# Two mixture-of-experts stages written out, with ring slots in turn, whole weight tiles, combination products moved earlier and GpSimd's share of the work moved to other engines

## The chip, the cores and the metric

One core of one Trainium2 chip runs the whole program. The metric is the device time of one execution in microseconds (us). The kernel before took 2744.36 us, the median of 3 runs (2743.35 to 2745.78).

## The reference, cut to what matters

A six-layer network on 256 tokens of width 1024, all in float32. The first two layers (a convolution mixer, then a differential attention beside a Hyena mixer) each end in an expert-choice feed-forward, the second four in a dense one. The change touches the two expert stages alone:

```python
def expert_choice_ffn(h, w_router, w_gate, w_up, w_down):
    aff = jax.nn.softmax((h @ w_router).astype(jnp.float32), axis=-1)
    g, idx = lax.top_k(jnp.swapaxes(aff, 1, 2), cap)          # cap = 32 tokens for each of 16 experts
    xe = jax.vmap(lambda hb, ib: hb[ib])(h, idx)
    a = jnp.einsum('becd,edf->becf', xe, w_gate)
    up = jnp.einsum('becd,edf->becf', xe, w_up)
    y = jnp.einsum('becf,efd->becd', jax.nn.silu(a) * up, w_down) * g[..., None].astype(h.dtype)
    return jax.vmap(lambda ib, yb: jnp.zeros((n, d), h.dtype).at[ib.reshape(-1)].add(yb.reshape(-1, d)))(idx, y)
```

In layer 0 it runs over two token sets (the sequence and its context, `ns = 2`) with the same weights, in layer 1 over one (`ns = 1`). Each expert has three 1024x1024 matrices, so each stage reads 16 x 12 MB = 201 MB of weights.

## The kernel before, in words

Each engine has its own program, and they meet by semaphores. A `Fill` is one use of a PSUM bank with a full and a free mark. A `Unit` is one use of a 2 MB weight slot, `[128, 4096]` floats; an expert has six: two halves each of gate, up and down. Seven slots form the ring (`RING = 7`). Stage 0 has one more slot in the arena for one unit only, stage 1 has two more for all of its units (9 slots). SyncE (SP) issues all weight transfers in the order of `stream`, and before each waits until the slot's former user is used up (`send`, L1461 whole, L1459 in pieces). It is one queue: a send that waits holds up all behind it. TensorE marks a half tile as used at `k == 3` (`moe_half`) and the other one with the bank's full mark.

**The head of a stage.** VectorE finds the top 32 tokens of each expert (L3007, L3008: maxima and replacement; L3011: what was taken; L3012: a running sum that numbers them; L3014), TensorE transposes that (L1591), VectorE makes the selection matrices `moe_sel` (L3026, one for each 128 tokens `t`). TensorE then gathers the tokens: `gather` (L1623) multiplies by the selections, once the rounded tokens `moe_hi` (ScalarE, L2433) and once the rest `moe_lo = moe_utok - moe_hi`. That rest is made by GpSimd (L3705) for the first two token chunks of a stage, and in stage 0 by VectorE (L3032) for chunks 2 and 3. Between, TensorE runs products of zeros (`fill_time`, L1195). By then the ring has been filled; nothing more can be sent until the first expert has used a tile.

**The experts.** `expert_pe`: gate products, up products (L1682, 32 instructions for each tile pair of gate or up), then silu (ScalarE L2448), the product with up (VectorE L3054), four transposes (L1694), a copy (L3056), down products (L1702). ScalarE copies the result to `moe_y` (L2465). Experts 0 to 3 are written out on all engines, 4 to 11 run in a loop of two rounds, 12 to 15 are written out again. In the looped part tokens are read from `x_cur`, to which GpSimd copies them (`put_x`, L3714). Banks alternate 0 to 3 and 4 to 7.

**Slots.** Units of four experts (24) form a round. In stage 0 a round uses slots 0 to 6 three times and then 2, 3, 4; in stage 1 slots 0 to 8 twice and then 1 to 6. Units 20 and 21 of a round (up of its last expert) come in 2 pieces of 1 MB, unit 23 (its last down tile) in 4 pieces of 512 KB, each with a semaphore of its own.

**The tail.** `weigh(q)` scales the results of experts 4q to 4q+3 by the gate value and splits them into `y_hi` and `y_lo` (L3074, L3077). `combine(s, b, qs)` (L1652) sends them back to the tokens of set `s`. The products of set 0 with q = 0, 1, 2 (48) stand between the half tiles of gate and up of expert 15 (`early`), the others behind expert 15. Then VectorE adds to `hT` (L3097). After stage 0 ScalarE issues four transfers of constants for Hyena (`hy_const`, L2586 to L2589), squares `hT` (L735) for the next norm, and TensorE sums the squares (L749). The first product that reads the constants is L1843.

Of the kernel before, what the change touches and what calls it, by code (L numbers as in the profile page):

```python
# [28 lines left out]
E = 16  # L29
# [201 lines left out]


# [38 lines left out]
def block_program(nc, a, out, LAST=8):  # L271

    with ExitStack() as ctx:
# [118 lines left out]
        def load(slots, sources, rounds=1, looped=True, first=0, sent=None):  # L392

            per = {s: slots.count(s) for s in set(slots)}
            seen = {s: 0 for s in per}
            got = []
            for s, (width, src) in zip(slots, sources):
                got.append(Unit(s, landed[s], slot_uses[s] + seen[s] - first * per[s], per[s] if rounds > 1 else 0,
                                width, src))
                seen[s] += 1  # L400
            for s in per:
                slot_uses[s] += per[s] * rounds
            stream.append((rounds, looped, first, [got[n] for n in sent] if sent else got))
            return got
# [43 lines left out]
        def plan_moe(l, ns):  # L448
# [11 lines left out]
            order = [n % n_slots for n in range(24 - 24 % n_slots)]  # L460
            order += [n + (2 if n_slots == RING else 1) for n in range(24 % n_slots)]
            units = []
            for j in range(4):
                units += [(SLOT, (lambda it, j=j, w=w, h=h: w[it * 4 + j, h]))
                          for w in (a["t_gate"][l], a["t_up"][l], a["t_down"][l]) for h in range(2)]
            early, sent, cleared = [slots[n] for n in order], None, plan["cd_out"][-1] if l else plan["ab_out"][-1]
            if l == 0:
                early = early[0:8] + [RING] + early[8:21] + [slots[2], slots[3]]
                sent = list(range(7)) + [8, 7] + list(range(9, 24))
            u0 = load(early, units, sent=sent)  # L470
            for slot in (RING, RING + 1):
                if slot in early:
                    u0[early.index(slot)].after = cleared.full
            us = load([slots[n] for n in order], units, 3, first=1)
# [6 lines left out]
            fs = fills(p + "experts", [0, 1, 2, 3, 4, 5, 6, 7] * 2, 3, first=1)  # L481
            for some, banks in ((u0, f0), (us, fs)):
                for j in range(4):
                    g, u, t, d = banks[4 * j:4 * j + 4]
                    for i, f in enumerate((g, u, d)):
                        some[6 * j + 2 * i].used = Mark(S("moe_half"), 48 * l + 3 * j + i + 1, 12)
                        some[6 * j + 2 * i + 1].used = f.full
            plan[p + "first"], plan[p + "first_units"], plan[p + "units"] = f0, u0, us
            for some, it in ((u0, 0), (us, 1)):
# [81 lines left out]
        if LAST >= 3:  # L571
# [11 lines left out]
            load_dots(0, 5)  # L583
# [783 lines left out]
        x_cur = region(18432, [2, KC, 2 * CAP])  # L1367
# [76 lines left out]
        def _(sp):  # L1444
# [18 lines left out]
            for rounds, looped, first, units in stream:  # L1463

                for u in units:
                    w = users.get(u.slot)
                    send(u, first, ([w] if w else []) + ([(u.after, 0)] if u.after else []))
                    users[u.slot] = (u.used, first)
                if rounds > 1:
# [11 lines left out]
                    if looped:  # L1481
                        with sp.Fori(first + 1, first + rounds) as it:
                            later(it)
                    else:
                        for it in range(first + 1, first + rounds):
                            later(it)
                    for s, u in last.items():
                        users[s] = (u.used, first + rounds - 1)
# [8 lines left out]
        def _(pe):  # L1497
# [44 lines left out]
            def moe_pe(l, ns):  # L1542
# [63 lines left out]
                def gather(half, sets):  # L1606

                    for s in sets:
                        if half == 0:
                            pe.wait_ge(S("moe_sel"), 4 * l + 2 * s + 2)  # L1610
                        for k0 in (0, 4):
                            for low in (0, 1):
                                if half == 0 and k0 == 0 and not low:
                                    pe.wait_ge(S("moe_hi"), 4 * l + 2 * s + 2)
                                elif half == 0 and k0 == 0:
                                    pe.wait_ge(S("moe_lo_late" if s else "moe_lo"), 2 if s else 2 * l + 2)
                                src = moe_lo[l] if low else moe_hi
                                for k in range(k0, k0 + 4):
# [39 lines left out]
                def expert_pe(j, it, first=False, beside=None):  # L1658

                    b = j % 2  # L1660
                    fs = plan[p + ("first" if first else "experts")]
                    us = plan[p + ("first_units" if first else "units")]
                    fg, fu, ft, fd = fs[4 * j:4 * j + 4]
                    un = us[6 * j:6 * j + 6]
                    if not first:
                        pe.wait_ge(S("x_cur"), 12 * l + j - 3 + it * 4)
                    for f, h0 in ((fg, 0), (fu, 2)):
                        f.open(pe, it)
                        for k in range(KC):
                            u = un[h0 + k // 4]  # L1670
                            if beside is not None and k % 4 == 0:
                                beside(h0 + k // 4)
                            landed_part(u, k % 4, it)
                            if first:
                                if j == 0 and h0 == 0 and k % 2 == 0:
# [2096 lines left out]
```

## Time and profile before

| | us |
|---|---|
| median of the runs | 2744.36 |
| the profiled execution, its own time | 2746.78 |
| its span | 2745.0 |
| around the span | 1.8 |
| TensorE busy | 2536.9 (92%) |
| VectorE busy | 1403.9 (51%) |
| ScalarE busy | 1012.0 (37%) |
| GpSimd busy | 32.3 (1%) |
| chain that ended last | PE 70%, DMA 19%, DVE 7%, ACT 2%, issue 2% |

The page names the engines PE (TensorE), PEld (its weight loads), DVE (VectorE), ACT (ScalarE), POOL (GpSimd) and SP (SyncE). Busy shares are over the whole span; the two expert stages (about 275 to 750 us and 996 to 1450 us) look different from the rest, since there the transfers run at 426 to 428 GB/s for most of the time.

### The profile page before, as it was taken

The page shows a single profiled execution, that of the slowest core. Times are in us where ns is not written, and L with a number is a line of the kernel's source. Part 1 is how long each engine was busy: PE and PEld are TensorE (multiplying, and loading weights), DVE is VectorE, ACT ScalarE, POOL GpSimd, SP SyncE. Part 2 cuts the span into 40 slices and gives each one's busy share as a digit, 9 for nine tenths or more (in the row PEclk, how much of TensorE's full clock was granted, in tenths as well). Part 3 has the DMA queues.
Part 4 walks back from the last instruction along what each step waited for, and adds up shares of the span by engine and source line. Part 5 has one row for each costly group of instructions (what it writes and reads, how often), then busy time and mean ns, then how long its engine had stood idle before and what let it go on. Part 6 is the DMA issues. An engine that isn't in the chain of part 4 may idle for free.

```text
span 2745.0 us, 33174 instructions
## 1 busy us (share of the span) xinstructions
PE 2536.9 (92%) x12537; PEld 1678.3 (61%) x12537; DVE 1403.9 (51%) x2437; ACT 1012.0 (37%) x1890; POOL 32.3 (1%) x45
## 2 busy tenths in 40 slices
PE   8999997777899999877789999999999999999999
PEld 5666432222465553322237788877888988887887
DVE  4988200001276530000124788668887468975776
ACT  5224111001121421000004656566565456655544
POOL 0000000000000000000000000000000000000000
PEclk9999999999999999999999999999999999999999
DMA  8767799999965369999994487616866418863242
GB/s 353 316 286 278 332 380 426 427 426 428 426 253 240 154 251 426 427 425 427 427 425 204 179 338 279 250 62 253 328 259 275 184 71 327 312 249 127 95 188 100
DMA packets 65268, 796.95 MB, mean 290 GB/s; under 512 B 9276, under 2 KB 10556, under 8 KB 15484
## 3 DMA queue, kind: packets, MB, share of 16 engines
q1 hardware_dynamic: 61424, 790.65, 70.3%
q10 hardware_dynamic: 3724, 4.66, 0.5%
q8 instruction: 80, 1.31, 0.2%
q14 instruction: 40, 0.33, 0.0%
HBM read 794.23 MB, written 1.05 MB: 290 GB/s over the span
## 4 chain that ended last, share of the span: by engine, by line
PE 70%; DMA 19%; DVE 7%; ACT 2%; issue 2%; SPq 0%; ACTq 0%; DVEq 0%
PE banks L2305 12%; PE banks L2316 9%; PE banks L1682 7%; DMA ring<-in_t_up 6%; DMA ring<-in_t_down 6%; PE banks L994 6%; DMA ring<-in_t_gate 6%; PE banks L1007 5%; PE banks L1702 5%; PE banks L2318 4%; PE banks L1761 3%; PE banks L1904 1%; PE banks L749 1%; PE banks L2028 1%; PE banks L871 1%
## 5 line engine op out<-in xcount | busy, mean ns | idle before, releaser
L1682 PE MATMUL banks<-ring,arena 128*64 128x512 f32 x1904 | 432.4, 600 | 84.5 <-DMA ring<-in_t_gate 45.3
L3054 DVE TENSOR_TENSOR arena<-arena,banks 128x512 f32<-128x512 f32 x32 | 22.0, 687 | 757.2 <-PE banks L1682 757.2
L2316 PE MATMUL banks<-u_pair,w_hi 128*128 128x512 f32 x1024 | 362.8, 399 | 1.7 <-DVE u_pair L1284 1.7
L3601 DVE TENSOR_TENSOR ring_lo<-ring,w_hi 128x1024 fp32r<-128x1024 f32 x256 | 311.8, 1220 | 99.1 <-ACT w_hi L2816 97.3
L1682 PEld LDWEIGHTS banks<-ring,arena 128*64 128x64 f32 x1904 | 138.9, 137 | 364.6 <-issue 263.3
L2816 ACT CAST w_hi<-ring 128x1024 fp32r<-128x1024 f32 x256 | 267.6, 1050 | 197.0 <-PE banks L2305 139.9
L2318 PE MATMUL banks<-u_pair,ring_lo 128*128 128x256 f32 x1024 | 287.6, 281 | 0.0
L2465 ACT COPY arena<-banks 32x512 f32<-32x512 f32 (+1 forms) x96 | 55.3, 576 | 499.1 <-PE banks L1702 498.2
L1702 PE MATMUL banks<-ring,arena 128*64 128x512 f32 x896 | 206.1, 608 | 28.3 <-DVE arena L3056 10.5
L2316 PEld LDWEIGHTS banks<-u_pair,w_hi 128*128 128x128 f32 x1024 | 192.4, 188 | 51.3 <-ACT arena L1254 3.7
L2305 PE MATMUL banks<-w_hi,ffn_h_hi 128*128 128x512 f32 x512 | 199.4, 389 | 0.0
L2305 PE MATMUL banks<-ring_lo,ffn_h_hi 128*128 128x512 f32 x512 | 199.4, 389 | 0.0
L2305 PE MATMUL banks<-w_hi,ffn_h_lo 128*128 128x512 f32 x512 | 199.2, 389 | 0.0
L2318 PEld LDWEIGHTS banks<-u_pair,ring_lo 128*128 128x128 f32 x1024 | 193.5, 189 | 0.5
L1290 ACT COPY arena<-banks 128x256 f32<-128x256 f32 (+2 forms) x222 | 92.9, 436 | 197.9 <-PE banks L1623 74.9
L1702 PEld LDWEIGHTS banks<-ring,arena 128*64 128x64 f32 x896 | 69.4, 139 | 146.9 <-issue 129.3
L3611 DVE SCALAR_TENSOR_TENSOR ring<-ring,hT 128x1024 f32<-128x1024 f32 x96 | 116.1, 1216 | 0.0
L1007 PE MATMUL banks<-uT_r,ring_lo 128*128 128x256 f32 x384 | 108.7, 283 | 0.0
L2448 ACT ACTIVATE arena<-banks 128x512 f32<-128x512 f32 x32 | 19.1, 597 | 242.5 <-PE banks L1682 242.5
L2305 PEld LDWEIGHTS banks<-ring_lo,ffn_h_hi 128*128 128x128 f32 x512 | 96.1, 188 | 20.3
L2305 PEld LDWEIGHTS banks<-w_hi,ffn_h_lo 128*128 128x128 f32 x512 | 96.1, 188 | 20.1
L2305 PEld LDWEIGHTS banks<-w_hi,ffn_h_hi 128*128 128x128 f32 x512 | 96.1, 188 | 19.3
(420 smaller groups left out, 4162.9 us busy)
## 6 DMA issues: line engine op xcount, KB each, us to landing
ring<-in_t_ffn SPq DMA_DIRECT2D x64, 2048.0 KB, 8.1
ring<-in_t_gate SPq DMA_DIRECT2D x60, 2048.0 KB, 29.4
ring<-in_t_ada_dots SPq DMA_DIRECT2D x54, 2048.0 KB, 9.7
ring<-in_t_down SPq DMA_DIRECT2D x48, 2048.0 KB, 28.6
ring<-in_t_up SPq DMA_DIRECT2D x43, 2048.0 KB, 30.3
ring<-in_t_ada SPq DMA_DIRECT2D x18, 2048.0 KB, 17.1
ring<-in_t_up SPq DMA_DIRECT2D x32, 1024.0 KB, 28.5
ring<-in_t_ret_in SPq DMA_DIRECT2D x12, 2048.0 KB, 8.0
```

The costliest lines, as they stand in the source:

```text
L994: mm = nc.tensor.matmul(PS[:, f.bank, :], x[:, ts], w, start=(q.first and k == 0 and step == 0), stop=(q.last and k == 1 and step == 2))
L1007: mm = nc.tensor.matmul(PS[:, f.bank, 0:N], w, x, start=(k == 0 and step == 0), stop=(k == KC - 1 and step == 2))
L1290: nc.scalar.copy(dst, src).then_inc(f.free.sem, 1)
L1682: mm = nc.tensor.matmul(PS[64 * h:64 * h + 64, f.bank, :], x, wview(u, 4)[:, k % 4, h * 512:(h + 1) * 512], start=(k == 0), stop=(k == KC ...
L1702: mm = nc.tensor.matmul(PS[64 * h:64 * h + 64, fd.bank, :], x_actT[:, b, fc % 4, (fc // 4) * 64:(fc // 4) * 64 + 64], wview(un[4 + fc // 4 ...
L1761: mm = nc.tensor.matmul(PS[:, fs[n].bank, :], w, x[:, k, :], start=(k == 0 and step == 0), stop=(k == KC - 1 and step == 2))
L2305: mm = nc.tensor.matmul(PS[:, f.bank, :], x[:, t * P:(t + 1) * P], w[:, m, :], start=False, stop=last and step == 2, skip_group_check=True)
L2316: nc.tensor.matmul(PS[:, f.bank, :], hi[:, q, :], u_pair[:, q].rearrange("p s t -> p (s t)"), start=(q == 0), stop=False, skip_group_check ...
L2318: mm = nc.tensor.matmul(PS[:, f.bank, 0:N], lo[:, q, :], u_hi[:, q, :], start=False, stop=(q == KC - 1), skip_group_check=True)
L2816: nc.scalar.copy(w_hi[:, n % 4], w).then_inc(S("ffn_w_hi"), 1)
L3601: TT(w_lo, w, w_hi[:, n % 4].bitcast(F32), ALU.subtract).then_inc(S("ffn_w_lo"), 1)
L3611: STT(w, w, 1.0, cond_rows[i], ALU.mult, ALU.mult, accum_out=dots[:, n:n + 1]).then_inc(S("dot"), 1)
```

## The change

- Slots in turn: unit n of a stage takes slot n modulo 7 (stage 0, shifted by one behind the arena's unit) or modulo 9 (stage 1), with no break at a round. All 96 sends are written out.
- No tile comes in pieces.
- TensorE's 16 experts and VectorE's are written out; experts 4 to 15 all use banks 0 to 3, the combination banks 4 to 7 (and 0 to 3 for set 1).
- The 48 combination products of set 0 with q = 0, 1, 2 move from expert 15 to experts 10, 11 and 13 (16 each), `weigh(0)` to `weigh(2)` to behind experts 9, 10 and 12 on VectorE.
- `x_cur` goes: products read `moe_xe` directly. In stage 1 a pair of experts' tokens (64 columns) is multiplied, and ScalarE reads the rows of the expert wanted.
- `moe_pool` goes. All of `moe_lo` is made by VectorE, two chunks at a time, directly behind the selections of these chunks. For the first token set TensorE gathers all eight `moe_hi` products before the `moe_lo` ones, where it went four by four.
- Hyena's constants are issued by SP behind the fourth tile of `dot_units`, with the same wait for the last combination.

```diff
-            order = [n % n_slots for n in range(24 - 24 % n_slots)]
-            order += [n + (2 if n_slots == RING else 1) for n in range(24 % n_slots)]
...
-            early, sent, cleared = [slots[n] for n in order], None, plan["cd_out"][-1] if l else plan["ab_out"][-1]
+            at, sent, cleared = [slots[n % n_slots] for n in range(96)], None, plan["cd_out"][-1] if l else plan["ab_out"][-1]
             if l == 0:
-                early = early[0:8] + [RING] + early[8:21] + [slots[2], slots[3]]
-                sent = list(range(7)) + [8, 7] + list(range(9, 24))
-            u0 = load(early, units, sent=sent)
+                at = at[0:8] + [RING] + at[8:95]
+                sent = list(range(7)) + [8, 7] + list(range(9, 96))
+            us = load(at, units, sent=sent)
...
-            fs = fills(p + "experts", [0, 1, 2, 3, 4, 5, 6, 7] * 2, 3, first=1)
+            fs = fills(p + "experts", [0, 1, 2, 3] * 4, 3, first=1)
...
-                for n, parts in ((20, 2), (21, 2), (23, 4)):
-                    some[n].parts = [Mark(S(f"piece{n}_{i}"), 16 * (4 * l + it + 1) - 16 * it, 16 * it)
-                                     for i in range(parts - 1)] + [some[n].landed]
-            fills(p + "combine", [0, 1, 2, 3, 4, 5, 6, 7][:4 * ns])
+            fills(p + "combine", [4, 5, 6, 7, 0, 1, 2, 3][:4 * ns])
@@ SP
+            def hyena_constants():
+                plan["moe0_combine"][-1].full.wait(sp)
+                sp.dma_start(hy_const, a["k_hyena"]).then_inc(S("hy_const"), 16)
...
+                    if u is plan["hy_const_behind"]:
+                        hyena_constants()
@@ TensorE, gather
-                        for k0 in (0, 4):
+                        span = KC if half == 0 and s == 0 else 4
+                        for k0 in range(0, KC, span):
@@ TensorE, expert_pe
+                    beside = {10: 0, 11: 1, 13: 2}.get(e)
+                    if beside is not None:
+                        pe.wait_ge(S("y_lo"), 8 * l + ns * beside + 1)
...
-                                beside(h0 + k // 4)
+                                combine(0, h0 + k // 4, (beside,))
...
-                                x = x_cur[:, b, k, :]
+                            x = moe_xe[l][:, e // 8, k, cs].rearrange("p e s c -> p (e s c)")
@@ ScalarE, result_act and after stage 0
-                            r = 64 * h + 32 * s
+                            r = 64 * h + 32 * (s if ns == 2 else j % 2)
...
-                act.dma_start(hy_const, a["k_hyena"]).then_inc(S("hy_const"), 16)
...
@@ VectorE
-                    if t == 3:
-                        for r in (2, 3):
+                    if t % 2:
+                        for r in (t - 1, t):
                             dve.wait_ge(S("moe_hi"), 4 * l + r + 1)
                             TT(moe_lo[l][:, r, :], moe_utok[l][:, r, :], moe_hi[:, r, :].bitcast(F32), ALU.subtract)\
...
@@ GpSimd
-            def moe_pool(l, ns):
...
```

## Rows read from the trace of the kernel before

**Rows 1.** Windows by stage: length, busy us (instructions) of each engine, PEclk, DMA share, GB/s.
```profile
284.70:404.00 119.30, 111.02 (x551) 46.77 (x552) 11.93 (x19) 18.41 (x32) 1.84 (x3) 1.00 0.92 382
404.00:713.00 309.00, 242.26 (x1072) 79.17 (x1072) 25.46 (x32) 31.31 (x54) 5.52 (x9) 0.99 1.01 427
1003.50:1124.70 121.20, 112.97 (x543) 45.88 (x544) 9.54 (x15) 11.58 (x20) 1.72 (x4) 1.00 0.97 408
1124.70:1401.00 276.30, 216.85 (x950) 70.79 (x948) 28.20 (x57) 18.80 (x34) 3.60 (x9) 0.98 1.01 427
```

**Rows 2.** Windows of 10 us in the first experts of stage 0, same columns.
```profile
350.00:360.00 10.00, 8.38 (x42) 3.21 (x38) 1.38 (x2) 0.00 (x0) 0.61 (x1) 1.00 0.90 373
360.00:370.00 10.00, 10.00 (x62) 5.82 (x60) 0.00 (x0) 4.45 (x8) 0.00 (x0) 1.00 0.65 227
...
380.00:390.00 10.00, 9.30 (x44) 3.86 (x46) 0.60 (x1) 2.14 (x4) 0.00 (x0) 1.00 0.95 372
```

**Rows 3.** Timeline of SP's queue in that stretch: start, us, what was issued.
```profile
344.33 4.24 SPq L1459 DMA_DIRECT2D ring<-in_t_up  x4
360.55 0.33 SPq L1461 DMA_DIRECT2D ring<-in_t_down  x1
```

**Rows 4.** Timeline of the head of stage 0: start, us, engine, line.
```profile
268.31 4.70 POOL L3705 TENSOR_TENSOR moe_lo<-arena,moe_hi 128x1024 fp32r<-128x1024 f32 x2 [159.43 <-ACT moe_hi L2433]
268.53 2.28 DVE L3011 TENSOR_SCALAR arena<-arena 32x256 f32<-32x256 f32 x1
270.85 2.71 DVE L3012 TENSOR_TENSOR_SCAN arena<-ones,arena 32x256 f32<-32x256 f32 x1
...
275.80 2.27 PE L1623 MATMUL banks<-moe_sel,moe_hi 128*128 128x256 f32 x8
276.80 2.35 DVE L3032 TENSOR_TENSOR moe_lo<-arena,moe_hi 128x1024 fp32r<-128x1024 f32 x2
...
284.74 7.09 PE L1682 MATMUL banks<-ring,arena 128*64 128x512 f32 x32
```

**Rows 5.** Timeline of the head of stage 1.
```profile
990.53 4.71 POOL L3705 TENSOR_TENSOR moe_lo<-arena,moe_hi 128x1024 fp32r<-128x1024 f32 x2 [239.65 <-ACT moe_hi L2433]
...
992.71 0.33 DVE L3011 TENSOR_SCALAR arena<-arena 16x256 f32<-16x256 f32 x1
993.07 2.71 DVE L3012 TENSOR_TENSOR_SCAN arena<-ones,arena 16x256 f32<-16x256 f32 x1
...
997.96 1.88 PE L1623 MATMUL banks<-hT_r,moe_hi 128*128 128x256 f32 x8 [0.19 <-DVE hT_r L3026]
...
1003.48 7.09 PE L1682 MATMUL banks<-ring,arena 128*64 128x512 f32 x32
```

**Rows 6.** Timeline of TensorE in experts 14 and 15 of stage 1; in brackets idle time and its cause.
```profile
1400.79 5.35 PE L1682 MATMUL banks<-ring,arena 128*64 128x512 f32 x16 [2.34 <-DMA ring<-in_t_up]
...
1427.54 3.65 PE L1682 MATMUL banks<-ring,arena 128*64 128x512 f32 x16
...
1432.75 3.65 PE L1682 MATMUL banks<-ring,arena 128*64 128x512 f32 x16
...
1438.68 7.09 PE L1702 MATMUL banks<-ring,arena 128*64 128x512 f32 x32 [0.83 <-issue]
```

**Rows 7.** Timeline of TensorE in expert 15 of stage 0.
```profile
713.05 3.65 PE L1682 MATMUL banks<-ring,arena 128*64 128x512 f32 x16 [0.19 <-DMA ring<-in_t_gate]
...
729.40 7.09 PE L1702 MATMUL banks<-ring,arena 128*64 128x512 f32 x32 [0.83 <-issue]
```

**Rows 8.** Timeline of TensorE behind stage 0: fill, norm sums, first use of the constants.
```profile
746.11 2.55 PE L1195 MATMUL banks<-zeros_bf 128*128 128x512 bf16 x11
749.39 5.77 PE L749 MATMUL banks<-arena,ones 128*128 128x512 f32 x12 [0.73 <-ACT arena L735]
...
774.02 0.64 PE L1843 MATMUL banks<-arena 33*64 33x256 f32 x2
```

**Rows 9.** Window of 1 us behind stage 0, columns as in rows 1.
```profile
770.00:771.00 1.00, 1.00 (x6) 0.87 (x6) 0.00 (x0) 0.00 (x0) 0.00 (x0) 1.00 0.35 147
```

More of the change, by code:

```diff
@@ L390, in fills, with load @@
             return got
-        def load(slots, sources, rounds=1, looped=True, first=0, sent=None):
+        def load(slots, sources, rounds=1, looped=True, sent=None):
             per = {s: slots.count(s) for s in set(slots)}
@@ L402, in load @@
                 slot_uses[s] += per[s] * rounds
-            stream.append((rounds, looped, first, [got[n] for n in sent] if sent else got))
+            stream.append((rounds, looped, [got[n] for n in sent] if sent else got))
             return got
@@ L1481, in _ @@
                     if looped:
-                        with sp.Fori(first + 1, first + rounds) as it:
+                        with sp.Fori(1, rounds) as it:
                             later(it)
                     else:
-                        for it in range(first + 1, first + rounds):
+                        for it in range(1, rounds):
                             later(it)
                     for s, u in last.items():
-                        users[s] = (u.used, first + rounds - 1)
+                        users[s] = (u.used, rounds - 1)
             for n, (half, t) in enumerate(BY_TOKENS):
@@ L1656, in combine, with expert_pe @@
                         mm.then_inc(f.full.sem, 1)
[L1658 to L1666, printed above, removed]
+                def expert_pe(e):
+                    beside = {10: 0, 11: 1, 13: 2}.get(e)
+                    if beside is not None:
+                        pe.wait_ge(S("y_lo"), 8 * l + ns * beside + 1)
+                    if beside == 0:
+                        for f in plan[p + "selT"]:
+                            f.free.wait(pe)
+                    j, it, b = e % 4, e // 4, e % 2
+                    first = it == 0
+                    fg, fu, ft, fd = plan[p + ("first" if first else "experts")][4 * j:4 * j + 4]
+                    un = plan[p + "units"][6 * e:6 * e + 6]
+                    if e == E // 2:
+                        for s in range(ns):
+                            for f in plan[p + f"gather1_{s}"]:
+                                f.free.wait(pe)
+                    cs = slice(e % 8, e % 8 + 1) if ns == 2 else slice(e % 8 - e % 2, e % 8 - e % 2 + 2)
                     for f, h0 in ((fg, 0), (fu, 2)):
@@ L1687, in expert_pe @@
                         mm.then_inc(f.full.sem, 1)
-                        if first and j == 0 and h0 == 0:
+                        if e == 0 and h0 == 0:
                             for t in range(0, TC * ns, TC):
@@ L1709, in expert_pe @@
                     mm.then_inc(fd.full.sem, 1)
[L1711 to L1729 removed]
+                for e in range(E):
+                    expert_pe(e)
+                    if 1 <= e <= ns:
+                        gather(1, [e - 1])
                 if ns == 2:
+                    pe.wait_ge(S("y_lo"), 6)
                     for b in range(3):
```

126 lines of the change are left out of this document (38 added, 88 removed).

## The prediction

> **What bounds the kernel now.** I read the page first (its chain puts TensorE ahead of DMA), then the windows by stage, because the averages hide that an expert stage has two halves. In the first experts TensorE is busy 111 of 119 us and the transfers don't fill their time; from expert 4 on the transfers run at 427 GB/s without a gap and TensorE is idle for 22% [rows 1]. So from there an expert lasts as long as its six tiles: 2.097 MB / 427 GB/s = 4.91 us each, 29.5 us for an expert, while TensorE needs 3 x 7.1 us and a chain of 2.3 us, 23.5 us [rows 4, 6]. What follows: a stage ends at the moment its first tile is used, plus 88 (87) tiles at full rate, plus each gap in the transfers, plus the work behind the last landing. An edit counts only in one of these four places. Then I looked for each.
>
> **1. The gap between the four-expert rounds.** Between 350 and 390 us the transfers fall to 373, 227 and 372 GB/s [rows 2]. Lost against 427: 54, 200 and 55 GB/s of 10 us each, that is 1.3 + 4.7 + 1.3 = 7.2 us (rounded sum). SP's queue shows why [rows 3]: after the pieces at 344 to 349 us its next send is at 360.5. This is unit 22, which goes to slot 2, and slot 2 was last given to unit 17, five units before; unit 17 is used up at 360.5. The next ones wait for 18, and 26 and 27 for 22 and 23. With slots in turn unit 22 waits for unit 15 and can go right behind 21. Going through all units of the first five experts with the times at which TensorE releases them, no slot is awaited longer than the transfers ahead of it last. Stage 0 gains 7.2 us, all of it, since TensorE has 6 us of slack an expert later. In stage 1 the distance is at least 7 already; its 408 GB/s in the early window [rows 1] is the startup: 5.7 us without transfers of 121. Gain 0. That the pieces themselves are slower than whole tiles can't be excluded: at 429 in place of 427 GB/s, two stages give 4 us, at no difference 0. I take 0.5.
>
> **2. The head.** A delay here moves the first release, thus the stage. In stage 0 VectorE's L3011 takes 2.28 us, the same line in stage 1 takes 0.33; both end 0.15 us after GpSimd's first subtraction (half of 4.70 us) ends. L3012 takes 2.71 us in both, and both times ends 0.55 us after GpSimd's second one [rows 4, 5]. I read this as VectorE being blocked by GpSimd's subtractions, which the change removes. L3011 falls to 0.33, gain 1.95 in stage 0 and 0 in stage 1. L3012: between 0.41 us (the L3014 product, same size) and its full 2.71. I take 0.55, the rest behind GpSimd's end; gain 2.16 in each stage.
> The Trainium skill, SBUF — State Buffer, section "Who interferes with whom", says that a VectorE instruction with two SBUF inputs, or in a two-port mode, is fully blocked by a GpSimd instruction that reads SBUF; the trace agrees as far as it goes, 2.28 against 0.33 us. The Trainium skill's page DVE: opcode table, instruction layouts, handler registers and perf-mode slots, section "Datapath and trigger behaviour", says that the scan runs at half throughput, so an estimate from it is some 0.5 us, near what I take.
>
> The added cost: VectorE now makes the first two `moe_lo` (2.35 us, L3032 [rows 4]) behind selection 1 and ahead of selection 2. TensorE has 16 `moe_hi` products first, at 0.13 us each (the 12 combinations between two half tiles take 1427.54 + 3.65 to 1432.75, 1.56 us, same shape [rows 6]): 2.1 us. It waits 0.3 us, and 2.1 us of `moe_lo` products end 4.5 us after the gather's start. Stage 1 is done there, against 5.5 us before [rows 5] (its first eight took 1.88 us, behind 2.25 us of idleness that shrinks to nothing). Gain 1.0. In stage 0 VectorE goes on with selections 2 and 3 (1.24) and two subtractions (2.35), ready at 5.9; then 24 products, 9.0 us in all, against 8.9 before [rows 4]: no gain. Bounds for it: +1.2 us if the wait falls away, -1 if the slow start stays. The gates `moe_selw` come some 1.5 us before their old time, nothing waits. Head of stage 0: 1.95 + 2.16 = 4.1 us. Stage 1: 2.16 + 1.0 = 3.2 us.
>
> **3. The tail.** Stage 1: up b of expert 14 lands at 1400.8, TensorE waited for it [rows 6]. The last down tile is eight tiles later, 1400.8 + 8 x 4.91 = 1440.1. But the down products end at 1445.8: TensorE lags, because 48 combination products stand between the half tiles, 1.56 us in each of four places. Without them up b (1430.3) is multiplied by 1433.9, the chain of 2.3 us leads to 1436.2, the first down half ends 1439.8, the second starts on the landing at 1440.1 and ends 1443.7. Gain 2.1 us. Whole tiles cost 2.7 us of what could be had here: with quarters only 0.9 us would stay behind the landing. Stage 0: gate b lands at 713.0 [rows 7], down b at 732.7, its products end at 736.4, against 736.5 before. There TensorE waited for gate b and then worked without pause to the end, so the pieces and the moved products just cancel: 0.1 us. The moved products are 16 in each of experts 10, 11 and 13, 2.1 us of the 6 us idle there: free. If that cover went, they would cost 6 us in each stage. Their wait for `y_lo` stands ahead of the gate products, and so holds up all of TensorE; `weigh` ends 4.1 us after the expert's copy, while 7.1 us of down products run. Single banks: the next expert opens bank 3 some 16 us after ScalarE began a copy of 2.4 us. Free too. `x_cur`'s copies on GpSimd were ahead of time: 0.
>
> **4. Behind stage 0.** ScalarE's four issues end at 748.5 and its first square is what L749 waits for, 0.73 us behind the end of the zeros at 748.66 [rows 8]. The zeros stay, so moving the issues gives 0.7 us (0 to 0.9). On SP the four issues and their wait hold up only the next tile, whose slot waits for the products at 760 to 767 anyway.
> The constants now come behind seven 2 MB tiles in one queue. They are needed at 774.0 [rows 8]; the seven tiles and the constants together were through at about 771 [rows 9], and that sum stays. So they land 1 to 2 us ahead of their use: 0, bounds 0 and -3 us.
> The Trainium skill, DMA: Bandwidth & Descriptors, "Queues, rings and completion order", says that an engine takes turns between queue rows; so ScalarE's queue got its share early, and SP's gives it last. This speaks against the move, and is the third rival.
>
> **The sum.** 7.2 + 0.5 + 4.1 + 3.2 + 2.1 + 0.1 + 0.7 = 17.9 us. The profiled execution took 2746.8 us (span 2745.0 and 1.8 around), so 2728.9 for the like of it; the median is 2.4 lower, so 2726.5 us. The four dense layers behind follow in TensorE's order and only shift.
>
> **The rivals.** What a measurement of this kernel can tell from no change is 0.2%, 5.5 us.
> First, the scan is simply 2.7 us long, and its end behind GpSimd's is a coincidence (both scans start as L3011 ends, so the two rows are no independent proof). Then both heads lose 2.2 us, and stage 1 keeps most of its idleness: gain 13, 2731.5 us. Chance 0.15.
> Second, the gap of 7.2 us comes back elsewhere: the transfers are no faster in sum because SP's queue meets another slot that is late, or TensorE in experts 4 to 6 is. Gain 10.7, 2733.7 us. Chance 0.08.
> Third, the constants land late and TensorE stands at L1843, which lies between its other products: up to 3 us, 2728 to 2730 us. Chance 0.12.
> Fourth, slower: written-out code reaches an engine too late, TensorE's or SP's, for the 16 experts that ran in a loop. TensorE's idleness of 6.4 us an expert must be used up, then all 17.9 us: from 17.9 / 16 + 6.4 = 7.5 us an expert on. At 8 us it gives 2735, at 9 us 2751 us. Experts 0 to 3 are written out already and TensorE is 93% busy in them [rows 1], which leaves no room for such a stall. Chance 0.04. Runtime: NRT & Kernel Launch of the Trainium skill, "Instruction fetch mechanics", would even have it the other way, taken branches stall.
> Fifth, no change to be measured, if rivals one to three meet: 0.03. Sixth, more gain (gather in stage 0, whole tiles at a better rate): 2719 to 2722, 0.04.
> My forecast has 0.54. The range: rivals one and two at the upper end with a us to spare, 2735; below the forecast 1.2 + 3.5 + some run scatter, 2720. Faster 0.93, same 0.03, slower 0.04.
>
> **What would show it.** L3012 at 0.5 to 0.6 us in both heads, the first expert product 4 and 3 us earlier counted from L3007; no window under 415 GB/s from the second release to the end of each stage; last down products starting on a DMA wait in both stages and ending 3.6 us later; no wait of L1843 on DMA. The prediction is wrong if `moe_lo` keeps TensorE waiting over 1 us, or a wait on `y_lo` appears ahead of experts 10, 11 or 13.

## The result, and the profile after

The changed kernel takes 2724.79 us (median of 4 runs, 2724.46 to 2725.91), the kernel before 2745.02 us beside it (2743.35 to 2745.78): ratio 0.9928, 95% interval 0.9911 to 0.9945. Its profiled execution took 2725.02 us with a span of 2723.2. The forecast was 2726.5 us.

The two traces are best compared in stretches that begin and end at the same piece of work. The table gives, in us, the head (from the first MAX8 of the dispatch to the first expert product) and the stage (from there to the end of the last down product) of both expert stages, and what lies between stage 0 and the first product with the Hyena constants.

| | head 0 | stage 0 | behind stage 0 | head 1 | stage 1 | sum |
|---|---|---|---|---|---|---|
| before | 20.05 | 451.75 | 37.53 | 14.61 | 442.29 | 966.23 |
| after | 15.82 | 443.75 | 36.29 | 11.37 | 439.25 | 946.48 |
| difference | -4.23 | -8.00 | -1.24 | -3.24 | -3.04 | -19.75 |
| predicted | -4.1 | -7.2 -0.25 -0.1 | -0.7 | -3.2 | -2.1 -0.25 | -17.9 |

The five together give 19.75 us. The medians differ by 20.2 us and the spans of the two profiled executions, from which the table comes, by 21.8. What lies outside the five stretches (the first 260 us above all, at whose end the profiled executions of all the kernels below are up to 5.4 us apart) is left out of every comparison below. Where a change is worth about a microsecond, these stretches decide and not the medians; each of them comes from one execution.

**The gap is closed.** Windows of the kernel after, first the two stages behind their startup, then the three 10 us windows in which the kernel before fell to 373, 227 and 372 GB/s [rows 2]; columns as there.

```profile
290.00:716.00 426.00, 355.73 (x1644) 130.28 (x1642) 35.57 (x48) 47.76 (x83) 0.00 (x0) 1.00 1.01 428
985.30:1401.00 415.70, 350.63 (x1605) 127.71 (x1604) 41.09 (x76) 31.62 (x56) 0.00 (x0) 1.00 1.00 422
...
350.00:360.00 10.00, 10.00 (x62) 5.96 (x59) 0.00 (x0) 2.69 (x5) 0.00 (x0) 1.00 1.00 424
360.00:370.00 10.00, 10.00 (x50) 3.37 (x48) 0.00 (x0) 2.36 (x5) 0.00 (x0) 1.00 1.01 429
...
380.00:390.00 10.00, 10.00 (x48) 3.96 (x46) 0.00 (x0) 2.90 (x5) 0.00 (x0) 1.00 0.99 423
```

Only the first window of a stage is lower (234 and 182 GB/s, from 280 and from 985 us on); of the windows of 10 us behind it none has under 419.

**The head.** Timeline of the kernel after in the heads of stage 0 and, behind the dots, of stage 1: start, us, engine, line, and in brackets idle time and its cause. They answer to [rows 4, 5]; the threshold L3011 of before is now L3000, the scan L3012 is L3001.

```profile
267.00 0.28 DVE L3000 TENSOR_SCALAR arena<-arena 32x256 f32<-32x256 f32 x1
267.31 0.68 DVE L3001 TENSOR_TENSOR_SCAN arena<-ones,arena 32x256 f32<-32x256 f32 x1
...
270.18 2.17 PE L1625 MATMUL banks<-moe_sel,moe_hi 128*128 128x256 f32 x16 [0.19 <-DVE moe_sel L3015]
272.31 1.28 DVE L3015 TENSOR_TENSOR moe_sel<-base,banks 128x512 fp32r<-128x512 f32 x2
272.45 2.18 PE L1625 MATMUL banks<-moe_sel,moe_lo 128*128 128x256 f32 x16
...
275.92 1.22 PE L1625 MATMUL banks<-moe_sel,moe_lo 128*128 128x256 f32 x8 [0.33 <-DVE moe_lo L3021]
...
278.99 7.09 PE L1690 MATMUL banks<-ring,arena 128*64 128x512 f32 x32
...
978.05 0.68 DVE L3001 TENSOR_TENSOR_SCAN arena<-ones,arena 16x256 f32<-16x256 f32 x1
...
985.27 4.94 PE L1690 MATMUL banks<-ring,arena 128*64 128x512 f32 x22
```

The scan fell from 2.71 to 0.68 us in both heads, the threshold from 2.28 to 0.28 in stage 0. Between the `moe_hi` and the `moe_lo` products TensorE loses 0.1 us: eight `moe_hi` products, two instructions each, just cover the two subtractions.

The shorter wait also changed TensorE's clock. Before, TensorE had stood idle for 2.25 us ahead of the gather of stage 1 (0.17 us after), and the kernel before has this window there:

```profile
998.00:1002.00 4.00, 4.00 (x21) 4.00 (x22) 1.28 (x3) 1.00 (x2) 0.00 (x0) 0.57 0.00 0
```

The granted clock was 0.57, most of the window at 1.2 GHz, and the first 16 instructions of the gather lasted 3.39 us (997.96 to 1001.35), where the kernel after needs 2.27 us for 16 (980.90 to 983.17) at a granted clock of 1.00.

**The tail.** TensorE of the kernel after at the ends of stage 0 and stage 1, which answer to [rows 7] and [rows 6].

```profile
709.31 3.65 PE L1690 MATMUL banks<-ring,arena 128*64 128x512 f32 x16 [1.14 <-DMA ring<-in_t_up]
713.75 0.66 PE L1702 MATMUL banks<-base,arena 128*128 128x128 f32 x4 [0.79 <-DVE arena L3043]
715.24 3.65 PE L1710 MATMUL banks<-ring,arena 128*64 128x512 f32 x16 [0.83 <-DVE arena L3045]
719.09 3.65 PE L1710 MATMUL banks<-ring,arena 128*64 128x512 f32 x16 [0.20 <-DMA ring<-in_t_down]
...
1411.08 3.65 PE L1690 MATMUL banks<-ring,arena 128*64 128x512 f32 x16 [1.15 <-DMA ring<-in_t_up]
...
1420.87 3.65 PE L1710 MATMUL banks<-ring,arena 128*64 128x512 f32 x16 [0.21 <-DMA ring<-in_t_down]
```

In both stages the last down tile's products now begin on that tile's landing and end 3.65 us later. Where the down products were one row of 7.09 us before, they are two with a wait between: the queue, not TensorE, sets the end.

**Behind stage 0.** TensorE of the kernel after, as in [rows 8], and then 1 us windows of the transfers, as in [rows 9].

```profile
732.38 2.55 PE L1189 MATMUL banks<-zeros_bf 128*128 128x512 bf16 x11
734.76 7.59 PE L743 MATMUL banks<-arena,ones 128*128 128x512 f32 x16
...
759.03 0.64 PE L1837 MATMUL banks<-arena 33*64 33x256 f32 x2
```

```profile
756.00:757.00 1.00, 1.00 (x7) 0.87 (x6) 0.00 (x0) 0.00 (x0) 0.00 (x0) 1.00 0.37 146
757.00:758.00 1.00, 1.00 (x6) 0.90 (x5) 0.00 (x0) 0.10 (x1) 0.00 (x0) 1.00 0.08 27
758.00:759.00 1.00, 1.00 (x6) 0.62 (x4) 0.59 (x2) 0.94 (x3) 0.00 (x0) 1.00 0.00 0
```

The norm's sums follow the zeros without the wait of 0.73 us. The constants' last bytes came between 757 and 758, and their product ran at 759.03 without a wait: they are 1 us ahead, as forecast, and no more than that.

### The profile page after: what moved, and what is told of

The parts are those of the page before. It is cut to its first block, busy times and chain, and to the rows that moved or that the text cites. A ratio compares the mean times of both kernels' runs of the same rounds, so it can differ in the third digit from the quotient of the medians.

```text
span 2723.2 us, 32687 instructions
## 1 busy us (share of the span) xinstructions
PE 2530.0 (93%) x12537; PEld 1676.5 (62%) x12537; DVE 1403.1 (52%) x2441; ACT 1011.9 (37%) x1890; POOL 10.3 (0%) x16
## 4 chain that ended last, share of the span: by engine, by line
PE 69%; DMA 20%; DVE 7%; ACT 2%; issue 2%; DVEq 0%; ACTq 0%
PE banks L2299 12%; DMA ring<-in_t_up 9%; PE banks L2310 9%; DMA ring<-in_t_down 8%; PE banks L1690 7%; PE banks L988 6%; PE banks L1001 5%; PE banks L2312 4%; PE banks L1710 4%; PE banks L1755 3%; DMA ring<-in_t_gate 3%; PE banks L1898 1%; PE banks L743 1%; PE banks L2022 1%; PE banks L865 1%
## 5 line engine op out<-in xcount | busy, mean ns | idle before, releaser
L1690 PE MATMUL banks<-ring,arena 128*64 128x512 f32 x1872 | 421.5, 596 | 77.8 <-DMA ring<-in_t_gate 39.2
L1710 PE MATMUL banks<-ring,arena 128*64 128x512 f32 x864 | 194.9, 596 | 25.9 <-DVE arena L3045 12.5
```

Of the source, the lines that this page charges most:

```text
L1690: mm = nc.tensor.matmul(PS[64 * h:64 * h + 64, f.bank, :], x, wview(u, 4)[:, k % 4, h * 512:(h + 1) * 512], start=(k == 0), stop=(k == KC ...
L1710: mm = nc.tensor.matmul(PS[64 * h:64 * h + 64, fd.bank, :], x_actT[:, b, fc % 4, (fc // 4) * 64:(fc // 4) * 64 + 64], wview(un[4 + fc // 4 ...
```

## The experiments

All kernels are the kernel after with one edit, unless said otherwise. Their times are medians of 4 or 5 runs (e6: one), beside the kernel before in the same series (9 runs each): 2743.04 us for e1 to e4, 2743.69 for e5 and e7 to e9, 2743.82 for e6 and e10 to e12. The stretches of the table above, from the profiled execution of each:

| | head 0 | stage 0 | behind | head 1 | stage 1 | median | ratio to before [95%] |
|---|---|---|---|---|---|---|---|
| e1_old_slots | 15.81 | 451.34 | 36.28 | 11.38 | 439.12 | 2732.63 | 0.9958 [0.9945, 0.9972] |
| e2_pieces | 15.83 | 444.46 | 36.27 | 11.38 | 439.72 | 2723.32 | 0.9924 [0.9911, 0.9938] |
| e3_down_pieces | 15.82 | 443.47 | 36.27 | 11.38 | 438.82 | 2722.87 | 0.993 [0.9916, 0.9943] |
| e4_combos_last | 15.82 | 444.66 | 36.29 | 11.38 | 440.17 | 2727.52 | 0.9941 [0.9927, 0.9954] |
| e5_gpsimd_lo | 21.09 | 443.93 | 36.27 | 14.58 | 439.26 | 2731.62 | 0.9957 [0.9942, 0.9973] |
| e6_memsets | 15.97 | 443.81 | 36.28 | 11.38 | 439.25 | 2724.84 (one run) | |
| e7_constants_act | 15.82 | 443.44 | 37.26 | 11.37 | 439.12 | 2726.24 | 0.994 [0.9924, 0.9955] |
| e8_gather_4 | 16.19 | 443.91 | 36.28 | 12.33 | 439.06 | 2726.07 | 0.9939 [0.9924, 0.9954] |
| e9_pieces_zeros | 15.81 | 442.50 | 37.03 | 11.38 | 437.91 | 2722.76 | 0.9926 [0.9913, 0.994] |
| e10_fill_2 | 15.82 | 443.84 | 35.13 | 11.38 | 439.14 | 2726.72 | 0.9934 [0.992, 0.9947] |
| e11_all | 15.82 | 442.86 | 36.85 | 11.37 | 438.15 | 2723.34 | 0.9921 [0.9908, 0.9935] |
| e12_all_ahead | 15.82 | 442.92 | 34.47 | 11.39 | 437.92 | 2721.04 | 0.9915 [0.9902, 0.9929] |

Stretches that an edit doesn't touch repeat within 0.25 us, with three exceptions of 0.3 to 0.4 (stage 0 in e7, and in e11 and e12 against e9). That is the measure for what follows.

**e1_old_slots: the slot order of before.**
```diff
-            at, sent, cleared = [slots[n % n_slots] for n in range(96)], ...
+            order = [n % n_slots for n in range(24 - 24 % n_slots)]
+            order += [n + (2 if n_slots == RING else 1) for n in range(24 % n_slots)]
...
+            at = at + [slots[n] for n in order] * 3
```


> The changed kernel with the old slot order in both stages (rounds of 24 units, with 2, 3, 4 or 1 to 6 at their ends), still whole tiles. My account: in stage 0 the windows between the second release and 390 us fall under 400 GB/s again, 7 to 8 us are lost there, none in stage 1: about 2732.5 us. Rival (the gap comes from the pieces or is made good later): within 2 us of 2724.8.


Stage 0 got 7.6 us longer, stage 1 not at all. The windows of 10 us from 350 to 390 in this kernel:

```profile
350.00:360.00 10.00, 10.00 (x61) 5.89 (x59) 0.00 (x0) 3.54 (x7) 0.00 (x0) 1.00 0.77 283
360.00:370.00 10.00, 10.00 (x50) 3.38 (x48) 0.00 (x0) 1.51 (x3) 0.00 (x0) 1.00 0.82 310
370.00:380.00 10.00, 8.38 (x42) 3.23 (x40) 1.38 (x2) 0.00 (x0) 0.00 (x0) 1.00 0.94 372
380.00:390.00 10.00, 10.00 (x48) 3.84 (x46) 0.00 (x0) 2.90 (x5) 0.00 (x0) 1.00 0.98 413
```

What is missing to 427 GB/s is 144 + 117 + 55 + 14 = 330, 330 x 10 / 427 = 7.7 us. So the whole gap is the slot order's, and what a gap in the queue costs is read from the windows: lost rate times time.

**e2_pieces, e3_down_pieces: the pieces of the last expert come back**, in e2 all of them, in e3 only those of the last down tile.
```diff
+            for n, parts in ((92, 2), (93, 2), (95, 4)):      # e3: ((95, 4),)
+                us[n].parts = [...] + [us[n].landed]
```


> The changed kernel with the last expert's up tiles in 2 pieces and its last down tile in 4, in both stages. Up b then ends 1.8 us earlier, the down products start on the landing of down a, and behind the last landing only a quarter tile is left, 0.9 us in place of 3.65: 2.7 us less for each stage, 2719.4 us. Rival (pieces cost rate or sending time as much as they give): 2724.8 us.

> The changed kernel with the last down tile alone in 4 pieces. By the sentence of the prediction (with quarters only 0.9 us stay behind the landing) 2.7 us less for each stage, 2719.4 us. By the trace after, in which the products of down a end only 0.2 us ahead of the last landing, 0.2 us less for each stage, 2724.4 us: the pieces of up are what makes those of down worth something.


Pieces of the last down tile alone gave 0.3 and 0.4 us, no more than the scatter. With all of them 2.7 us were expected in each stage, and both stages came out longer, by 0.7 and 0.5. TensorE at the end of stage 0 in e2, and its windows of 4 us:

```profile
707.37 1.94 PE L1692 MATMUL banks<-ring,arena 128*64 128x512 f32 x8 [0.54 <-DMA ring<-in_t_up]
710.10 0.66 PE L1704 MATMUL banks<-base,arena 128*128 128x128 f32 x4 [0.79 <-DVE arena L3045]
712.36 8.78 PE L1712 MATMUL banks<-ring,arena 128*64 128x512 f32 x32 [1.61 <-DMA ring<-in_t_down]
```

```profile
708.00:712.00 4.00, 1.96 (x12) 0.56 (x6) 1.38 (x2) 0.00 (x0) 0.00 (x0) 1.00 0.99 403
712.00:716.00 4.00, 3.64 (x12) 1.43 (x14) 0.00 (x0) 0.00 (x0) 0.00 (x0) 0.65 1.07 436
716.00:720.00 4.00, 4.00 (x20) 1.54 (x18) 0.00 (x0) 0.00 (x0) 0.00 (x0) 0.93 1.01 427
```

The pieces did what they should: the chain ended early, and TensorE then stood 1.61 us before the down products. But it had been busy for only 1.96 of 4 us, and the granted clock fell to 0.65 and 0.93 in the next windows, part of them at 1.2 GHz; 32 products took 8.78 us in place of 7.09, in both stages. This is one execution, the slowest of five. The median of e2, 2723.32 us, is within 0.5 us of that of e3 in the same series, and its ratio to the kernel before, 0.9924, is no worse than the 0.9928 of the kernel after, so how often the clock falls there is open.

**e9_pieces_zeros: e2 with products of zeros in these waits.**
```diff
+                    if e == E - 1:
+                        fd.open(pe, it)
+                        fill_time(fd, 3)          # ahead of the transposes; 7 more ahead of the down products
```


> The kernel with pieces for up and down of the last expert, plus 3 products of zeros ahead of that expert's transposes and 7 behind them. If the gain of the pieces was lost because TensorE stood idle there and ran the down products at a lower granted clock, they now take 7.1 us in place of 8.8, and a stage is 2.2 to 2.7 us shorter than with whole tiles (441.2 us and 436.7 us from first expert product to last down product), 4 to 5 us in all. Rival (pieces land later in sum): no gain, 443.8 and 439.3 us.


TensorE and its windows in e9:

```profile
709.09 1.67 PE L1191 MATMUL banks<-zeros_bf 128*128 128x512 bf16 x7
710.90 7.09 PE L1717 MATMUL banks<-ring,arena 128*64 128x512 f32 x32
```

```profile
708.00:712.00 4.00, 3.83 (x20) 1.71 (x20) 1.23 (x2) 0.00 (x0) 0.00 (x0) 1.00 1.01 410
712.00:716.00 4.00, 4.00 (x20) 1.56 (x18) 0.00 (x0) 0.00 (x0) 0.00 (x0) 1.00 1.04 425
```

The clock stays at 1.00 and the products at 7.09 us: the fall in e2 came of the idleness, and it cost 1.7 us. The gain against the kernel after is 1.25 and 1.34 us, half of what was expected (0.8 to 1.3 us in e11 and e12, which have the same edit). The rest is bounded by another landing: in e2, where TensorE waited for the first down tile, it was used 435.7 us into stage 0; in e9 the down products start at 435.4, right behind the zeros, and take 7.1 us from then. The expectation had counted from the last tile's last quarter.

**e4_combos_last: the 48 combination products go back into expert 15.**
```diff
-                    beside = {10: 0, 11: 1, 13: 2}.get(e)
+                    beside = 0 if e == E - 1 else None
...
-                                combine(0, h0 + k // 4, (beside,))
+                                combine(0, h0 + k // 4, (0, 1, 2))
```


> The changed kernel with the 48 combination products back in expert 15, tiles whole. 1.56 us more ahead of each half tile against 1.2 us of idleness there: TensorE falls 1.1 us behind the landings in each stage, 2727.0 us. Rival (they are covered there too): 2724.8 us.


The stages are 0.91 and 0.92 us longer, near the 1.1 that was expected.

**e5_gpsimd_lo: GpSimd makes the first two `moe_lo` again**, with VectorE's copy of that work left out.
```diff
+                for r in range(TC):
+                    pool.wait_ge(S("moe_hi"), 4 * l + r + 1)
+                    nc.gpsimd.tensor_tensor(moe_lo[l][:, r, :], moe_utok[l][:, r, :], ..., ALU.subtract)...
```


> The changed kernel with the first two moe_lo of each stage made by GpSimd again, VectorE making those of chunks 2 and 3 in stage 0 as before. My account (GpSimd's subtractions block VectorE): the running sum goes from 0.68 back to 2.7 us in both heads, L3000's threshold to 2.3 us in stage 0, and the time from the first maximum to the first expert product from 15.8 and 11.4 us to 20.0 and 14.6 us: 7 us more in all. Rival (the head got shorter because of the order of the gather or the written-out code): both lengths stay within 1 us.


Head of stage 0 in e5:

```profile
265.52 4.70 POOL L3702 TENSOR_TENSOR moe_lo<-arena,moe_hi 128x1024 fp32r<-128x1024 f32 x2 [158.49 <-ACT moe_hi L2432]
265.73 2.28 DVE L3005 TENSOR_SCALAR arena<-arena 32x256 f32<-32x256 f32 x1
268.05 2.71 DVE L3006 TENSOR_TENSOR_SCAN arena<-ones,arena 32x256 f32<-32x256 f32 x1
...
273.37 3.94 PE L1630 MATMUL banks<-moe_sel,moe_hi 128*128 128x256 f32 x16
```

Both durations of before are back to the hundredth, in a program that is otherwise the new one. Head 0 takes 21.09 us, though, where 20.0 was expected and 20.05 measured before. TensorE had again been idle for 4.49 us, the granted clock was 0.50 from 273.3 to 277.1, and now all 16 `moe_hi` instructions stand there: 3.94 us in place of 2.17. The wait for the scan thus costs twice, once itself and once in the clock of what comes behind it.

**e6_memsets: GpSimd runs eight memsets of 128x512 in that place**, which compute nothing.
```diff
+                for i in range(8):
+                    nc.gpsimd.memset(region(20480, [512]), 0.0).then_inc(S("pool_set"), 1)
```


> The kernel after, where in both experts' heads GpSimd runs eight memsets of 128x512 fp32 (all to one piece of the arena that nothing else uses then, one after another) while VectorE does the threshold and the scan of the dispatch; nothing is left out. It asks which of GpSimd's instructions hold VectorE up. Theory: only those that read and write for a share of the port (moe_lo's subtraction, with two operands, did: with it the threshold took 2.28 and the scan 2.71 us, without it 0.28 and 0.68), and a memset, which reads nothing, leaves the scan at 0.68 us (0.65 to 0.75). By the lock of the Trainium skill, SBUF - State Buffer, section Who interferes with whom, too, the scan would not be held up by a write-only instruction. Rival: any GpSimd instruction that runs beside them holds them up, and the scan takes 1.2 us or more (until the memset that runs then has ended). Time: the head gets longer only by what VectorE waits for the last memset before it makes the selection matrices.


Head of stage 0 in e6:

```profile
264.84 4.63 POOL L3698 MEMSET arena<- 128x512 f32 x8 [158.49 <-ACT moe_hi L2427]
265.08 0.42 DVE L3000 TENSOR_SCALAR arena<-arena 32x256 f32<-32x256 f32 x1
265.54 0.68 DVE L3001 TENSOR_TENSOR_SCAN arena<-ones,arena 32x256 f32<-32x256 f32 x1
```

GpSimd is as busy as in e5, and the scan takes 0.68 us, as without it. The threshold, with one input, took 0.42 in place of 0.28: held up for at most the rest of one memset (0.58 us each). In the head of stage 1 both ran beside the memsets at 0.28 and 0.68 us. So it is not GpSimd's activity that stops the scan but what its instruction does. The Trainium skill, SBUF — State Buffer, section "Who interferes with whom", says that a VectorE instruction with two SBUF inputs is blocked by a GpSimd instruction that reads, not by one that only writes; the pair e5 and e6 agrees (2.71 against 0.68 us), and so does the threshold if it ran in one of the two-port modes that the section names, which no row here shows.

**e7_constants_act: ScalarE issues the constants again.**
```diff
+                act.dma_start(hy_const, a["k_hyena"]).then_inc(S("hy_const"), 16)       # and the three behind it
```


> The changed kernel with Hyena's constants issued by ScalarE behind the last combination, as before. From the end of stage 0's down products to the first product that reads the constants: 37.5 us, as before the change, in place of 36.3. Rival (the 1.2 us came from the banks of the combination): 36.3 us stays.


It is 1.0 us longer behind stage 0, of the 1.24 that the change had won there: TensorE waits again for the first square, here 0.74 us:

```profile
734.26 7.67 PE L743 MATMUL banks<-arena,ones 128*128 128x512 f32 x16 [0.74 <-ACT arena L729]
```

**e8_gather_4: the gather goes four by four again.**
```diff
-                        span = KC if half == 0 and s == 0 else 4
+                        span = 4
```


> The changed kernel with the gather of the first token set four by four again, while VectorE still makes all of moe_lo. TensorE then waits for moe_lo after 1.0 us of products, not after 2.1: from the first maximum to the first expert product 1 us more in stage 1 (12.4), 0.5 to 0.8 in stage 0 (16.5). Rival (another wait hides it): no change in either.


The head of stage 1 gets 0.96 us longer, that of stage 0 0.37. TensorE in head 1:

```profile
982.91 1.21 PE L1625 MATMUL banks<-hT_r,moe_lo 128*128 128x256 f32 x8 [1.05 <-DVE moe_lo L3021]
```

With VectorE as the maker of `moe_lo`, the wide gather is what hides it. This prices a wait that the change would have added without the wide gather; the kernel before, where GpSimd had `moe_lo` ready, had no such wait.

**e10_fill_2, e11_all, e12_all_ahead: how near the constants are.** e10 runs 2 products of zeros behind stage 0 in place of 11. e11 adds that to e9. e12 is e11 with the constants issued one tile earlier.
```diff
-                fill_time(plan["hy_in"][0], 11)
+                fill_time(plan["hy_in"][0], 2)
...
-            plan["hy_const_behind"] = dot_units[3]
+            plan["hy_const_behind"] = dot_units[2]            # e12 alone
```


> The kernel after, with two products of zeros in place of eleven behind stage 0 (they fill TensorE's time before the norm's sums; they compute nothing). In the kernel after, they ran from 732.38 to 734.93 us, and the norm's first two squares were ready at 733.25, so that the sums could start up to 1.5 us earlier. Theory: TensorE's chain from stage 0's last down product to the first use of the Hyena constants gets 1.0 to 1.5 us shorter (36.3 to 34.8 to 35.3 us), which is held back where the constants have not landed: in the kernel after, their transfer's rate had fallen to 87 GB/s from 756 to 758 and the product ran at 759.03 without a wait, so some 1 to 1.5 us are to be had. Time: 1.0 to 1.5 us below the kernel after. Rivals: the squares of the later chunks come too late, the sums wait for them, and nothing is won (36.3); or TensorE's granted clock falls in the gap and it gets longer (over 37).

> The kernel after with up a, up b and down b of the last expert in pieces, products of zeros in its waits (3 and 7), and two products of zeros in place of eleven behind stage 0. Theory: stages as with pieces and zeros (442.5 and 437.9), but nothing more behind stage 0, since there the constants bind: with pieces and zeros the first product that needs them waited 0.68 us for their landing (37.03 us behind the stage), and with fewer zeros it waits 2.2 us for the same landing (still 37.0). Time: that of pieces and zeros, 2.5 us below the kernel after by the stages less 0.7 behind stage 0. Rival: the wait moves with TensorE, or comes from elsewhere, and 35.5 us remain behind stage 0.

> The run with pieces, zeros and two products of zeros behind stage 0, and besides SyncE issues the Hyena constants ahead of the fourth tile of the ada dots (behind the third), not behind it. Theory: the constants then land a tile earlier (a tile took 4.9 us), the product that needs them no longer waits, and the stretch behind stage 0 is 34.8 to 35.5 us: 1.5 to 2.2 us less than in the run where they are sent behind the fourth tile. Time: 3.5 to 4.5 us below the kernel after. Rival: the fourth tile of the dots, now held until stage 0's last combination product, comes late and TensorE waits for it instead (37 us or more, or as much lost behind it).


The first product with the constants, in e9:

```profile
755.02 0.61 PE L1844 MATMUL banks<-arena 33*64 33x256 f32 x2 [0.68 <-DMA arena<-in_hf_w]
```

in e10:

```profile
759.87 0.61 PE L1837 MATMUL banks<-arena 33*64 33x256 f32 x2 [0.58 <-DMA arena<-in_hf_w]
```

in e11:

```profile
759.95 0.61 PE L1844 MATMUL banks<-arena 33*64 33x256 f32 x2 [2.32 <-DMA arena<-in_hf_w]
```

and in e12:

```profile
755.04 0.64 PE L1844 MATMUL banks<-arena 33*64 33x256 f32 x2
```

e10 gains 1.16 us in its stretch, then stands for the constants. Its median, 2726.72 us, doesn't show the gain; its profiled execution began 1.9 us later than that of the kernel after, and whether that is all of it stays open. e11 gains nothing behind the stage over e9 (36.85 against 37.03), since the earlier start of TensorE only lengthens the wait, from 0.68 to 2.32 us. e12 takes the wait away: 34.47, and 2721.04 us (2720.55 to 2721.91), 2.3 us below e11 in the same series. Its five stretches sum to 942.52 us, 3.96 below the kernel after; the medians, from two series, differ by 3.75. It is the fastest version found.

## Why the prediction was right

It was right to 1.7 us, and each of the larger terms has its experiment or its rows. The forecast gained 17.9 us, the measurement 20.2; the terms below say where the difference lies. All five stretches gained a little more than was forecast, so nothing cancelled by luck; only in stage 1's tail does the term stand on a wrong cause.

- **The gap between rounds**, 7.2 us: e1 gives 7.6. What was put down as lost rate in [rows 2] was all there was, and nothing came back (second rival: fell).
- **Scan and threshold**, 1.95 + 2.16 and 2.16 us: 2.00 + 2.03 and 2.03 by the rows. The reading that GpSimd blocked VectorE held (e5, e6), and the first rival, a scan that is simply 2.7 us long, fell. Its length was taken as 0.55 and is 0.68 us.
- **The gather in stage 1**, 1.0 us: 3.24 less the scan's 2.03 and the threshold's 0.05 leaves 1.2. It is the slow start that went away, as forecast: the first 16 instructions lasted 3.39 us before, mostly at 1.2 GHz, and 2.27 after, 1.1 us less. That `moe_lo` by VectorE added no wait is the wide gather's doing (e8, 0.96 us).
- **Stage 0's tail and its half of the pieces' rate**, 0.1 and 0.25 us: 8.00 less 7.6 leaves 0.4, which is as large as the scatter of a stage. Whether the pieces' rate is worth anything isn't shown; nor has the change of banks or the loss of `x_cur` a run of its own.
- **Behind stage 0**, 0.7 us: 1.24, of which e7 shows 1.0 for the issues. The wait of 0.73 was priced, and not that the stretch as a whole follows; under-sized by 0.5 us; what the other 0.2 us are is open.
- **The constants (third rival).** They came 1 us ahead, so it did not happen. e9 to e11 show that it was the right one to fear, and its price: 0.6 to 2.3 us as soon as TensorE comes earlier. The Trainium skill's rule of turns between queue rows (DMA: Bandwidth & Descriptors, "Queues, rings and completion order") spoke against SP's queue: with ScalarE's queue (e7) there was no wait for the constants either (the last bytes came between 756 and 757 us, the product ran at 758.60), so the runs neither bear it out nor refute it.
- **Written-out code (fourth rival):** TensorE waits for tiles in experts 14 and 15, not for instructions, and no 10 us window of a stage behind its first has under 419 GB/s. It fell. Its two times were added up wrongly, too: 7.5 us an expert is where all the gain is gone, 2744.4 us, so 8 us would give 2752 and 9 us 2768, not 2735 and 2751.

Two steps were wrong, although the sum held.

First, stage 1's tail. The 2.1 us were put down to the combination products. Putting them back costs only 0.9 us (e4). Between expert 14's up b and the last down products the kernel before lost another 1.3 us, and its windows there show what [rows 6] show in one duration, 5.35 us for 16 products that took 3.65 elsewhere:

```profile
1396.00:1400.00 4.00, 2.45 (x12) 0.69 (x8) 0.00 (x0) 0.00 (x0) 0.00 (x0) 1.00 1.02 426
1400.00:1404.00 4.00, 3.21 (x8) 0.93 (x10) 0.00 (x0) 0.00 (x0) 0.00 (x0) 0.62 1.00 426
1404.00:1408.00 4.00, 2.79 (x14) 0.95 (x10) 1.01 (x2) 0.00 (x0) 0.00 (x0) 0.95 1.01 430
```

TensorE had idled 2.34 us for that tile, the granted clock fell to 0.62, and of the 1.7 us lost 1.3 were never made up, because behind it the 48 products filled the waits. In e4 the same products took 3.65 us, and from their start to that of the last down products it needs 36.56 us, against 37.89 before. The last 0.8 of the 3.04 us are the landing of this tile: up b was used 397.3 us into the stage before and 396.5 after. It came late by itself, for the tile ahead of it (up a, kernel before) was used 391.3 us into the stage, earlier than the 391.7 of the kernel after:

```profile
1394.79 3.65 PE L1682 MATMUL banks<-ring,arena 128*64 128x512 f32 x16 [1.33 <-DMA ring<-in_t_up]
```

From there to 1400.79 are 6.0 us, where two tiles are else 4.8 to 5.0 apart. The prediction counted its eight tiles from this late one. Counted from the tile ahead of it the same sum is 1394.79 + 9 x 4.91 + 3.65 = 1442.6, a gain of 3.1 us, and 3.04 were measured. Why that tile was late is open. That the lower clock met expert 14 in one execution is seen; how often it does in others is not. The kernel after has such a place too, in stage 1 from 1259.26 on (2.07 us idle, then 16 products in 5.35 us), but in an expert in which the idleness behind it takes the loss up.

Second, "whole tiles cost 2.7 us of what could be had here: with quarters only 0.9 us would stay behind the landing". This is wrong. Quarters of the last tile are worth at most 0.3 to 0.4 us (e3), since the products of both down tiles run 7.1 us without a pause from where the chain has ended. All pieces lose 0.5 to 0.7 where the clock falls (e2), and with the clock held 0.8 to 1.3 us can be had (e9, e11, e12), up to the landing of the first down tile. Pieces of that tile too weren't tried.

## What to carry to other kernels

Where one queue feeds a stage, find each window under the full rate and turn it into time; then ask what the last instruction there waited for, because only gaps, the first release and the work behind the last landing count. Before you let an engine finish earlier, look at what lands next and by how much: here 1 us of room was all, and the next gain needed the transfer moved first (e11 against e12). And before you cut work into pieces that wait for transfers, look at the granted clock: a shorter chain that leaves TensorE idle can cost more in its clock than the pieces give. The same holds for any wait ahead of TensorE's work: its price is the wait and what follows it at the lower clock (head 0 of e5).

## What the runs showed of the hardware

- A GpSimd subtraction with two SBUF inputs held up a VectorE scan (2.71 against 0.68 us) and a threshold with one input (2.28 against 0.28 us) until it had ended; with eight memsets in the same place the scan took 0.68 us.
- TensorE's granted clock fell to 0.65 and 0.62 in the 4 us behind stretches in which it was busy for 1.96 of 4 and 2.45 of 4 us (e2 from 708, and the kernel before from 1396). In e9, with zeros in the waits, it was busy 3.83 of 4 us and stayed at 1.00. It isn't every such idleness: the kernel after was busy 2.32 of 4 us from 1384 to 1388 and had 1.00 there and in the next window (the 32 products behind it took 7.45 us in place of 7.09; why, at that clock, isn't shown).
- The clock also fell behind the waits of the heads: 0.57 from 998 to 1002 in the kernel before, behind 2.25 us of idleness, and 0.50 from 273.3 to 277.1 in e5, behind 4.49 us.
- With nothing sent behind them, the last bytes of the constants came slowly: behind 385 to 453 GB/s the transfers of the kernel after ran at 244, 206, 146 and 27 GB/s in the last 4 us, and a product waits for the last of them.
